# State space section of a two-block network: finer waits on the gate, and one weight split moved behind it

## The reference

```
proj      = rms_norm(x) @ ssm_in_w          # z | x, B, C | dt
x, B, C   = silu(causal_conv4(x | B | C))   # xs 256, B 128, C 128 columns per group
dt        = softplus(dt + bias);  a = -exp(A_log) * dt;  a_cum = cumsum in chunks of 128
per chunk c of 128 tokens and per head:
  Y_diag  = (C B^T * exp(a_cum_i - a_cum_j), lower triangle) @ (x * dt)
  state   = state * exp(a_cum_end) + B^T (x * dt * exp(a_cum_end - a_cum))
  Y_off   = C state_before * exp(a_cum)
y         = (Y_diag + Y_off + D * x) * silu(z);  rms_norm over the group;  out = y @ ssm_out_w
```

## Time and profile before

| | us |
|---|---|
| median of three runs | 1752.11 (1751.29 to 1752.52) |
| profiled execution, own time | 1751.73 |
| its span, first to last instruction | 1749.9 |
| mean granted TensorE clock | 0.994 of full |

### The profile page before, as it was taken

The page is one execution under the profiler, slowest core; times in us unless marked ns, Lnnn a source line. Parts: engine busy times, 40 slices in busy tenths (PEclk is TensorE's granted clock), DMA queues, the critical chain, the costliest instruction groups (busy, mean ns, idle before and its releaser), DMA issues.

```text
span 1749.9 us, 23401 instructions
## 1 busy us (share of the span) xinstructions
PE 1705.8 (97%) x9024; PEld 1378.1 (79%) x9024; DVE 879.6 (50%) x1757; ACT 768.1 (44%) x1311; POOL 751.2 (43%) x1001
## 2 busy tenths in 40 slices
PE   8999899999999999999989999999999999999998
PEld 8977667877888888887877777877788777787876
DVE  6498863434631212126656666066554554445355
ACT  6554743632642323214354445155445453435343
POOL 5464412422455555541455556565441333323330
PEclk9999999999999999999999999999999999999999
DMA  8422001211222222221211222221221212112201
GB/s 304 160 97 97 25 1 49 97 48 49 93 100 96 97 96 97 97 85 49 97 51 70 73 73 73 86 70 42 75 81 50 98 50 74 51 50 86 85 1 49
DMA packets 25814, 136.50 MB, mean 78 GB/s; under 512 B 2623, under 2 KB 7999, under 8 KB 12008
## 3 DMA queue, kind: packets, MB, share of 16 engines
q1 hardware_dynamic: 25704, 135.02, 22.6%
HBM read 132.88 MB, written 2.12 MB: 77 GB/s over the span
## 4 chain that ended last, share of the span: by engine, by line
PE 78%; DVE 10%; ACT 9%; issue 2%; DMA 0%; SPq 0%; DVEq 0%; ACTq 0%
PE ps L1422 75%; PE ps L1426 3%; ACT whi L1898 2%; ACT tmp L1898 1%; ACT L1898 1%; ACT ESG L1898 1%; DVE GY L2324 1%; DVE XS L2324 1%; DVE BL L2747 1%; ACT XS L1898 1%; ACT ZS L1898 1%; ACT ECG L1898 1%; DVE ESG L2713 1%; DVE LG L2324 0%; PE ps L1430 0%
## 5 line engine op out<-in xcount | busy, mean ns | idle before, releaser
L2820 POOL TENSOR_TENSOR wlo<-raw,whi 128x256 fp32r<-128x256 f32 (+1 forms) x916 | 671.7, 770 | 830.1 <-ACT whi L1898 830.1
L1898 ACT ACTIVATE whi<-raw 128x2048 fp32r<-128x2048 f32 (+4 forms) x135 | 231.2, 1718 | 193.6 <-PE ps L1422 186.4
L1422 PE MATMUL ps<-XH,whi 128*128 128x512 f32 (+1 forms) x1176 | 299.6, 375 | 4.0 <-ACT XH L1898 3.9
L1422 PE MATMUL ps<-XL,whi 128*128 128x512 f32 (+1 forms) x1176 | 282.4, 362 | 0.1
L1422 PE MATMUL ps<-XH,wlo 128*128 128x512 f32 (+1 forms) x1176 | 281.1, 361 | 0.0
L1422 PEld LDWEIGHTS ps<-XH,whi 128*128 128x128 f32 x1176 | 202.0, 190 | 43.5 <-ACT XH L1898 6.4
L1422 PEld LDWEIGHTS ps<-XL,whi 128*128 128x128 f32 x1176 | 205.8, 190 | 35.3 <-DVE XL L2386 0.3
L1422 PEld LDWEIGHTS ps<-XH,wlo 128*128 128x128 f32 x1176 | 205.2, 189 | 34.1
L2416 DVE TENSOR_TENSOR R<-ps,R 128x512 f32<-128x512 f32 (+1 forms) x128 | 79.9, 625 | 267.0 <-PE ps L1422 266.1
L1422 PE MATMUL ps<-BH,whi 128*128 128x512 f32 (+1 forms) x480 | 132.2, 392 | 1.2 <-ACT BH L1898 1.2
L1422 PE MATMUL ps<-BL,whi 128*128 128x512 f32 (+1 forms) x480 | 125.5, 377 | 0.8 <-DVE BL L2747 0.8
(11 more groups left out here) (313 smaller groups left out, 2750.1 us busy)
## 6 DMA issues: line engine op xcount, KB each, us to landing
raw<-wall SPq DMA_DIRECT2D x107, 1024.0 KB, 4.7
raw<-wall SPq DMA_DIRECT2D x11, 512.0 KB, 3.5
raw<-wall SPq DMA_DIRECT2D x8, 576.0 KB, 3.7
raw<-wall SPq DMA_DIRECT2D x4, 768.0 KB, 4.1
BFL<-scr SPq DMA_DIRECT2D x2, 1024.0 KB, 6.8
outT<-R SPq DMA_DIRECT2D x16, 128.0 KB, 1.8
MEM<-memT SPq DMA_DIRECT2D x2, 512.0 KB, 5.0
XTA<-x SPq DMA_DIRECT2D x2, 512.0 KB, 9.4
```

Source lines behind the costliest of these rows:

```text
L1422: return nc.tensor.matmul(o_, l, r_, start=start, stop=stop, skip_group_check=True)
L1898: return nc.scalar.activation(o_, i_, func, bias=bias, scale=scale)
L2820: t = tt(wlo[u % NSPL][:, c], raw[u % NRAW][:, c], f32(whi[u % NSPL][:, c]), ALU.subtract)
```

## The change

Four waits are altered and one step is moved. PE's single wait for all of the gate becomes three: for two signals before the turns of XS, for three before the turn of BT, for four before the product of CTs and BT. POOL's wait before the ECG product becomes four signals. DVE gets a new wait for the whole gate in front of `g2`. And the `split` put in the order at the end of group 1's `xs` projection is held back until right behind `gate(0)`.

```diff
-        def unit_done(lo="g_lo"):
+        held = []
+
+        def unit_done(lo="g_lo", hold=False):
+
             at[0] += 1
             u = at[0] + NSPL - 1
             if u < len(units):
                 low[u] = lo
-                emit("split", u)
-
-        def project(key, tiles, K, meta=None):
+                held.append(u)
+                if not hold:
+                    release()
+
+        def release():
+            while held:
+                emit("split", held.pop(0))
+
+        def project(key, tiles, K, meta=None, hold=False):
...
-            unit_done()
+            unit_done(hold=hold)
...
         def group_in(g):
             if g:
-                yield from project("xs", 2, 8, g)
+                yield from project("xs", 2, 8, g, g == 1)
...
                 emit("gate", 0)
+                release()
                 next(main)
                 scan = scans(0)
...
-                e.wait_ge(*on("a_gate", "gate", g))
+                e.wait_ge(*on("a_gate", "gate", g, i=2))
                 tr(o_[:, 0:128], xs[:, 0, cc])
                 tr(o_[:, 128:256], xs[:, 1, cc])
+                e.wait_ge(*on("a_gate", "gate", g, i=3))
                 tr(o_[:, 256:384], bt[:, cc]).then_inc(S("p_ga"), 1)
                 o_ = taken(e, "cb", g, c)
+                e.wait_ge(*on("a_gate", "gate", g, i=4))
                 mm(o_[:, 0:128], bt[:, cc], ct_[:, cc], True, True).then_inc(S("p_cb"), 1)
...
                 gy = taken(e, "GY", g)
+                e.wait_ge(*on("a_gate", "gate", g))
...
-                    e.wait_ge(*on("a_gate", "gate", g))
+                    e.wait_ge(*on("a_gate", "gate", g, i=4))
```

## The result

The changed kernel is slower. Against the kernel before in the same job its ratio is 1.0022 (95% interval 1.0014 to 1.0030; medians of 12 executions 1755.64 and 1751.16 us); a second job gave 1.0013 (1.0005 to 1.0022; 1754.05 and 1751.18 us). The forecast was 1751.8 us, between 1748.8 and 1755.2, with a chance of 0.80. The profiled execution of the changed kernel took 1753.28 us, its span is 1751.5 us. PE's busy time is 1702.6 us against 1705.8 and the clock 0.994 again, so neither tells anything about the change.

The account below looks back on a forecast made before the run. PE, busy 97% of the span, was taken to bound the kernel, so only its pauses could pay. 1751.7 + 3.1 - 2.9 - 0.2 = 1751.7 us, put at 1751.8; range 1748.8 to 1755.2.

Parts of the forecast that it names:

- First group: At the first gate, PE's pause moves to XDE behind POOL's eight subtractions: 3.1 us slower, bounds +1.4 to +5.1.
- Last group: At gate 7, finer waits gain 1.5 us and 1.4 us of lost clock: -2.9 us, bounds -1.5 and -3.2.
- Groups 1 to 6: At the middle gates, PE's 0.29 us pauses go but are mostly given back: -0.2 us, bounds -1.7 and +0.5.
- None of those steps starts earlier by the change: Groups 1, 2, 3 and 5: chain without PE keeps its times, so the 0.29 us is given back.
- group 4: At its gate, the chain leaves through PE, so finer waits gain; at most 0.6 us together with group 6.
- group 6: At its gate, the chain leaves through PE, so finer waits gain; at most 0.6 us together with group 4.
- Rival B: Groups 1, 2, 3, 5: gate and state pauses merge, the clock falls, 1.7 us each: +6.8, 1758.5 us; chance 0.04.
- the state waits: In the middle groups, PE's wait for the state product grows from 0.42 to 0.7 us.
- The rule on the drain: ACT table loads: 1.38 us of drain per load would make the sum 1.4 us higher; nothing was added.
- The rule on the shared interface: GpSimd contends with VectorE's two-SBUF-input instructions: subtractions in the first group priced at 5.51 us, 6.21 at the upper bound.

Follow-up runs that it names:

- hold_only: The changed kernel with PE waiting for all six signals of the gate again, the split still moved; ratio to the kernel before 1.0017.
- late_release: The changed kernel with the held split released behind the first two turns in place of in front of them; ratio to the kernel before 0.9988.
- middle_only: The changed kernel with the split back in front of the gate and PE's finer waits in groups 1 to 6 alone; ratio to the kernel before 1.0002.
- pool_wait2: The changed kernel with GpSimd's subtractions for bc of group g+2 waiting for VectorE's product on the state (g = 1, 2, 3, 5); ratio to the kernel before 1.0001.
- after_again: The changed kernel once more, nothing edited, for a second profile; ratio to the kernel before 1.0013.

## Why the prediction was wrong, step by step

**First group: mechanism right, size near.** Forecast +3.1, measured +3.71 and +2.88. XDE was late by 1.45 us against 1.4; the pause was 6.04 us, inside 4.7 to 6.4. Only the clock is off: 2.3 us lost behind the pause in one profile, 1.5 in the other, against 1.7. hold_only shows the same harm alone and late_release shows it go when XDE stands in front.

**Last group: right in the pairs of profiles, partly by luck.** Forecast -2.9, measured -2.91 and -2.94. But 1.5 us of it (35.0 against 33.46) is a fall of the clock that the old wait brought in two of four profiles. The prediction took that fall, seen in the one profile that it had, for a fixed cost of the wait. Where it does not happen the finer waits give 1.4, less than the lower bound of 1.5.

**Groups 1 to 6: the step that failed.** I wrote that "None of those steps starts earlier by the change", and took -0.2, bounded by +0.5. Measured +1.55: +0.53, +0.53, +0.51 and +0.48, -0.49 in group 4, and nothing in group 6. It is true that ScalarE's silus did not start earlier; but measured against VectorE's chain the copy of whi, behind a pass that waits for PE's projection, came 0.20 us sooner, and with it GpSimd, and GpSimd slows a VectorE product in the chain. I had followed the chain that set the end and asked what releases its pieces, not what runs beside them and how long they take. middle_only shows the term alone, pool_wait2 takes 0.37 of 0.53 away by adding only a wait on GpSimd. In group 4 the product on the state is slowed too (0.95 us for 0.41) and costs nothing, because the chain there is PE's. The chain of the earlier trace rows has some 70 pieces when all are counted, and not 27; that none is PE's holds. Rival B named the right groups for the wrong cause: the state waits did grow, to 1.4 us and not the 0.7 forecast, and the clock stayed at 1.00 behind them in both profiles.

Group 4 gave 0.49, more than the 0.29 that the wait showed. PE's last four matmuls before the gate started 1.36 us ahead of the first turn before (1058.05 to 1059.41), and 0.91 after (1062.49 to 1063.40): the modelled end of a matmul hides part of a pause, and 0.45 is what it was. Group 6, for which the same was forecast, gave nothing: there the chain that ended last leaves the gate through PE before, and through ScalarE and VectorE after.

**The sum.** With the measured terms +3.3 (mean of 3.71 and 2.88), +1.6 and, as the mean of -2.9 and -1.4 for a last gate with and without the old fall, -2.1, the change costs 2.8 us. The two timings say 4.5 and 2.9 us by medians, 3.9 and 2.3 by ratios. So the failed term (1.8 us off) and the clock at the last gate (0.8 us) account for 2.6 us of a miss of 2.3 to 3.9 by the ratios. The forecast sat at zero because two terms near 3 us cancelled, and a term of 1.6 decided the sign. Its own bounds add up to 1751.7 + 5.1 - 1.5 + 0.5 = 1755.8 at the top, more than the 1755.2 given. The mean granted clock, which is kept for every execution, tells something of the rest. In 72 later executions of the kernel before it was 0.995 or more in 35 (mean 1750.6 us) and 0.993 or less in 29 (1753.0). In the 23 of the changed kernel it was so in 7 (1753.4) and 14 (1755.1). At a like clock the change costs 2.8 and 2.1 us, and the lower clock came more often with it. Where the clock falls in those executions stays open, since none near 1756 us was profiled.

The rule on the drain (the Trainium skill, "ScalarE: Activation LUTs", section "What ACT_TABLE_LOAD costs"), which I had set aside, added nothing in the run: whi starts 1.29 us after the second table load starts. The rule on the shared interface, in "GPSIMD Engine Reference" of the Trainium skill, section "1. Specifications", names a contention with VectorE instructions that have two SBUF inputs. The traces agree with it, and I had priced it for GpSimd's side only. VectorE's product pays too, 0.94 us for 0.41, when GpSimd is first.

## What to carry to other kernels

A step that is moved takes the work of every queue with it: look in each queue for what stands behind it, and for who waits for that, the slow engine first. Before a finer wait is put everywhere, read in the chain which stages leave through it (here groups 0, 4 and 7); in the others the time comes back as another wait, and what is moved forward may meet something that it missed before. Where the whole time scatters more than the effect, measure between fixed marks inside the program.

## What the runs showed that I had not expected

The product STT and DEC of VectorE, 128x256 with both inputs in SBUF, takes 0.41 us when it starts 0.07 to 0.09 us ahead of GpSimd's subtractions, and 0.94 to 0.95 us when it starts 0.10 to 0.12 us behind them. This holds for the first such product of groups 1, 2, 3 and 5 in every profile in which GpSimd has no added wait. GpSimd's eight subtractions take 5.50 us beside convolution passes and up to 6.5 beside VectorE work with two SBUF inputs. A difference of 0.2 us in starts decides which engine is held up.

The cost of a clock fall is not a constant of the pause. Behind pauses of 6.0 to 6.1 us it was 2.3 us in the first profile of the changed kernel, 1.4 in pool_wait2 and 1.5 in after_again; behind the same 1.9 us pause it was 1.5 us in two profiles and nothing in two. In late_release the clock fell behind a pause of 1.1 us and one of 0.3; right behind the same two pauses it did not fall in the eight other profiles that have them.
